# Attention rows without the first softmax's denominator, and the second softmax's factor made on GpSimd, in a two-layer hybrid encoder on one core

## The reference, cut to what matters

```python
s = jnp.einsum('bqhcd,bkhcd->bhcqk', qblk, kh) * scale
p = jax.nn.softmax(s, axis=-1)
p_diff = p[:, :, 0] - lam * p[:, :, 1]
o = jnp.einsum('bhqk,bkhv->bqhv', p_diff, vh)
...
o = rmsnorm(o, subln_g) * (1.0 - lam_init) * jax.nn.silu(g)
# rmsnorm(x, g) = x * rsqrt(mean(x * x) + 1e-6) * g
```

## Time and profile before

| what | value |
|---|---|
| median of 3 runs | 1490.94 us (1490.22 to 1490.95) |
| profiled execution: its time | 1490.54 us |
| profiled execution: span of its instructions | 1488.7 us |
| TensorE matmul busy | 1471.9 us, 11216 instructions |
| VectorE busy | 1047.2 us, 1787 instructions |
| ScalarE busy | 836.1 us, 1768 instructions |
| GpSimd busy | 90.5 us, 109 instructions |
| chain that ended last | TensorE 96%, VectorE 1%, ScalarE 1%, issue 1% |
| granted TensorE clock | 1.0 of full speed, over the whole span |

### The profile page before, as it was taken

The page is one execution under the profiler, slowest core; times in us unless marked ns, Lnnn a source line. Parts: engine busy times, 40 slices in busy tenths (PEclk is TensorE's granted clock), DMA queues, the critical chain, the costliest instruction groups (busy, mean ns, idle before and its releaser), DMA issues.

```text
span 1488.7 us, 28116 instructions
## 1 busy us (share of the span) xinstructions
PE 1471.9 (99%) x11216; PEld 1402.6 (94%) x11216; DVE 1047.2 (70%) x1787; ACT 836.1 (56%) x1768; POOL 90.5 (6%) x109
## 2 busy tenths in 40 slices
PE   7999999999999999999999999999999999999998
PEld 7999999999999999999999999999999889999987
DVE  7777667776664777777576676767776657777754
ACT  6565555665433565566555555566654445665654
POOL 0000000000000000000100000000001000000010
PEclk9999999999999999999999999999999999999999
DMA  6112111111223222222232121121212232222222
GB/s 208 63 53 66 64 58 57 58 57 58 76 68 89 84 72 72 72 66 67 69 101 86 57 72 57 62 68 57 71 58 72 72 104 82 72 72 82 76 84 73
DMA packets 34562, 109.94 MB, mean 74 GB/s; under 512 B 4864, under 2 KB 4992, under 8 KB 34432
## 3 DMA queue, kind: packets, MB, share of 16 engines
q1 hardware_dynamic: 34432, 108.15, 23.3%
HBM read 97.38 MB, written 2.10 MB: 67 GB/s over the span
## 4 chain that ended last, share of the span: by engine, by line
PE 96%; DVE 1%; ACT 1%; issue 1%; DMA 0%; SPq 0%; DVEq 0%; ACTq 0%
PE proj L1556 65%; PE pair L1674 8%; PE meta L1784 4%; PE pair L1769 2%; PE pair L1771 2%; PE main L1798 2%; PE meta L1786 1%; PE main L1739 1%; PE pair L1720 1%; PE main L1740 1%; PE main L1652 1%; PE main L1681 1%; PE main L1743 1%; PE pair L1727 1%; PE pair L1706 0%
## 5 line engine op out<-in xcount | busy, mean ns | idle before, releaser
L1556 PE MATMUL proj<-u_hi,w_hi 128*128 128x264 f32 (+1 forms) x2048 | 495.2, 313 | 9.0 <-DVE w_lo L1082 7.8
L1556 PE MATMUL proj<-u_hi,w_lo 128*128 128x264 f32 (+1 forms) x2048 | 465.6, 299 | 0.0
L1556 PE MATMUL proj<-u_lo,w_hi 128*128 128x264 f32 (+1 forms) x2048 | 465.3, 298 | 0.0
L1556 PEld LDWEIGHTS proj<-u_hi,w_hi 128*128 128x128 f32 x2048 | 327.2, 190 | 21.5 <-DVE w_lo L1082 7.8
L1556 PEld LDWEIGHTS proj<-u_hi,w_lo 128*128 128x128 f32 x2048 | 326.3, 189 | 11.2
L1556 PEld LDWEIGHTS proj<-u_lo,w_hi 128*128 128x128 f32 x2048 | 326.6, 189 | 7.7
L1082 DVE TENSOR_TENSOR w_lo<-w_raw,w_hi 128x1024 fp32r<-128x1024 f32 x178 | 218.9, 1230 | 51.3 <-ACT w_hi L682 51.3
L904 ACT ACTIVATE decay<-pair,neg_max 128x528 f32<-128x528 f32 (+1 forms) x144 | 100.3, 696 | 218.3 <-DVE neg_max L1423 218.1
L682 ACT ACTIVATE w_hi<-w_raw 128x1024 fp32r<-128x1024 f32 x178 | 186.6, 1049 | 53.0 <-PE proj L1556 51.8
L1423 DVE TENSOR_REDUCE neg_max<-pair 128x1 f32<-128x528 f32 (+1 forms) x144 | 101.4, 704 | 110.5 <-PE pair L1771 110.4
L1674 PE MATMUL pair<-q_level,qk_dec 128*128 128x128 f32 x896 | 121.4, 278 | 0.0
(11 more groups left out here) (216 smaller groups left out, 2214.4 us busy)
## 6 DMA issues: line engine op xcount, KB each, us to landing
w_raw<-w_units SPq DMA_DIRECT2D x178, 512.0 KB, 3.5
q_stack<-gate_f SPq DMA_DIRECT2D x32, 132.0 KB, 2.3
k_stack<-k_stack SPq DMA_DIRECT2D x32, 132.0 KB, 2.3
h<-x_t SPq DMA_DIRECT2D x8, 264.0 KB, 5.6
cos_sin<-rope SPq DMA_DIRECT2D x2, 528.0 KB, 6.1
out_t<-ops SPq DMA_DIRECT2D x2, 512.0 KB, 3.5
out_t<-decay SPq DMA_DIRECT2D x2, 512.0 KB, 3.9
masks<-level_masks SPq DMA_DIRECT2D x1, 448.0 KB, 6.4
```

The source lines that it names most:

```text
L1556: ins = pe.matmul(out, w, x[:, tile, cols_n], start=(k == 0 and p == 0), stop=(k == last_k and p == 2))
```

## The change

The copy of the attention result no longer scales a row by 1 / s0; for the attention heads the epsilon that invert_rms adds is multiplied by s0 squared, row by row (`square_sums`, into `eps_sums`). The factor -lam s0 / s1 is made on GpSimd (`relate_sums`: s1 to the power of -1, then times lam and s0), and VectorE waits for it (`ratio_ready`) where it made it itself. `row_sum` holds a head's sums for all blocks, twice, so that square_sums finds them. GpSimd's queue in an attention head becomes: relate_sums of block 0, cut_mixed of the head before, relate_sums of the other blocks, square_sums, invert_rms. Two memsets come at the start. The sums are set to 1.0 at the start, which is what stays where a block has no row.

```diff
@@ -365,14 +365,16 @@
         minus_half = sb("minus_half", [P, N_CHUNKS + 1])
+        minus_one = sb("minus_one", [P, 1])
         mixed_t = sb("mixed_t", [P, T])
...
         neg_max = sb("neg_max", [P, 2, 2])
-        row_sum = sb("row_sum", [P, 2, 2])
-        row_inv = sb("row_inv", [P, 2, 2])
+        row_sum = sb("row_sum", [P, 2, 2, N_CHUNKS + 1])
+        sum_ratio = sb("sum_ratio", [P, 2])
+        eps_sums = sb("eps_sums", [P, N_CHUNKS + 1])
 
@@ -480,6 +487,10 @@
 
+        def attended(n):
+
+            return n // HEADS * AT_HEADS + n % HEADS - HG_HEADS
+
         def evac_count(t):
@@ -632,22 +643,57 @@
             pool.memset(minus_half[:, :], -0.5).then_inc(ones_set, 1)
+            pool.memset(minus_one[:, :], -1.0).then_inc(ones_set, 1)
             pool.memset(v_meta[:, :], 0.0).then_inc(pads_set, 1)
...
             pool.memset(k_low[:, :, :].bitcast(f32), 0.0).then_inc(pads_set, 1)
+            pool.memset(row_sum[:, :, :, :], 1.0).then_inc(pads_set, 1)
 
...
                     pool.wait_ge(o_scaled, n)
-                pool.tensor_scalar(o_inv[:, :], o_sums[:, :], P * NORM_EPS, None, ALU.add)\
-                    .then_inc(pool_step, 1)
+                if n % HEADS < HG_HEADS:
+                    pool.tensor_scalar(o_inv[:, :], o_sums[:, :], P * NORM_EPS, None, ALU.add)\
+                        .then_inc(pool_step, 1)
+                else:
+                    pool.wait_ge(eps_ready, attended(n) + 1)
+                    pool.tensor_tensor(o_inv[:, :], o_sums[:, :], eps_sums[:, :], ALU.add)\
+                        .then_inc(pool_step, 1)
                 pool.wait_ge(pool_step, n + 1)
                 pool.tensor_tensor(o_inv[:, :], o_inv[:, :], minus_half[:, :], ALU.pow)\
                     .then_inc(o_inv_ready, 1)
+
+            def relate_sums(n, j):
+
+                l, a = n // HEADS, attended(n)
+                at = before(a, 5, AT_HEADS) + j
+                r = slice(0, P if j < N_CHUNKS else N_META)
+                if n == HG_HEADS and j == 0:
+                    pool.wait_ge(lam_ready, 1)
+                pool.wait_ge(exp_done, 2 * at + 2)
+                if at >= 2:
+                    pool.wait_ge(p_ready, at - 1)
+                s0, s1 = (row_sum[r, a % 2, comp, j:j + 1] for comp in range(2))
+                ratio = sum_ratio[r, at % 2:at % 2 + 1]
+                pool.tensor_tensor(ratio, s1, minus_one[r, :], ALU.pow).then_inc(sum_inverted, 1)
+                pool.wait_ge(sum_inverted, at + 1)
+                pool.tensor_scalar(ratio, ratio, lam[r, l:l + 1], s0, ALU.mult, ALU.mult).then_inc(ratio_ready, 1)
+
+            def square_sums(n):
+
+                a = attended(n)
+                pool.wait_ge(exp_done, 2 * before(a + 1, 5, AT_HEADS))
+                if a > 0:
+                    pool.wait_ge(pool_step, n)
+                sums = row_sum[:, a % 2, 0, :]
+                pool.tensor_tensor(eps_sums[:, :], sums, sums, ALU.mult).then_inc(sums_squared, 1)
+                pool.wait_ge(sums_squared, a + 1)
+                pool.tensor_scalar(eps_sums[:, :], eps_sums[:, :], P * NORM_EPS, None, ALU.mult)\
+                    .then_inc(eps_ready, 1)
 
@@ -657,10 +703,18 @@
             for l in range(DEPTH):
-                for c in range(HEADS):
+                for c in range(HG_HEADS):
                     n = l * HEADS + c
                     if c > 0:
                         cut_mixed(n - 1)
+                    invert_rms(n)
+                for c in range(HG_HEADS, HEADS):
+                    n = l * HEADS + c
+                    relate_sums(n, 0)
+                    cut_mixed(n - 1)
+                    for j in range(1, query_chunks(l)):
+                        relate_sums(n, j)
+                    square_sums(n)
                     invert_rms(n)
@@ -903,7 +957,7 @@
                                    ACT.Exp, bias=neg_max[0:rows, i % 2, comp:comp + 1],
-                                   accum_out=row_sum[0:rows, i % 2, comp:comp + 1]).then_inc(exp_done, 1)
+                                   accum_out=row_sum[0:rows, a % 2, comp, i:i + 1]).then_inc(exp_done, 1)
                 if s == 1:
@@ -913,8 +967,7 @@
                     act.wait_ge(pv_done, chunks_before + j + 1)
-                    inv = row_inv[0:rows, j % 2, 0:1]
-                    act.activation(o_rows[0:rows, j, :], meta[0:rows, 0:P], ACT.Copy, scale=inv)\
+                    act.activation(o_rows[0:rows, j, :], meta[0:rows, 0:P], ACT.Copy)\
                         .then_inc(pv_read if j < chunks - 1 else o_taken, 1)
@@ -947,8 +1000,8 @@
 
-            act.wait_ge(ones_set, 4)
-            act.wait_ge(pads_set, 5)
+            act.wait_ge(ones_set, 5)
+            act.wait_ge(pads_set, 6)
             load_root_table()
@@ -1072,9 +1125,10 @@
                                            math.sqrt(P) * (1.0 - init) * 0.5, None, ALU.mult))
-                step(dve.tensor_scalar(g_hg[:, :], g_hg[:, :], math.sqrt(P), None, ALU.mult))
+                dve.tensor_scalar(g_hg[:, :], g_hg[:, :], math.sqrt(P), None, ALU.mult).then_inc(lam_ready, 1)
                 w = step(dve.tensor_scalar(g_final[:, :], g_final[:, :], math.sqrt(D_MODEL), None, ALU.mult))
                 after(w)
+                dve.wait_ge(lam_ready, 1)
 
@@ -1438,18 +1492,12 @@
                     r = slice(0, P if j < 4 else N_META)
-                    dve.wait_ge(exp_done, 2 * chunks_before + 2 * j + 2)
-                    w = step(dve.reciprocal(row_inv[r, j % 2, :], row_sum[r, j % 2, :]))
-                    after(w)
-                    w = step(dve.scalar_tensor_tensor(row_inv[r, j % 2, 1:2], row_inv[r, j % 2, 1:2],
-                                                      lam[r, l:l + 1], row_sum[r, j % 2, 0:1],
-                                                      ALU.mult, ALU.mult))
                     if j >= 2:
                         dve.wait_ge(p_turned, chunks_before + j - 1)
-                    after(w)
+                    dve.wait_ge(ratio_ready, chunks_before + j + 1)
 
                     e0, e1 = decay[r, 2 * (j % 2), :], decay[r, 2 * (j % 2) + 1, :]
-                    dve.scalar_tensor_tensor(qk_dec[r, j % 2, 0, :], e1, row_inv[r, j % 2, 1:2], e0,
+                    dve.scalar_tensor_tensor(qk_dec[r, j % 2, 0, :], e1, sum_ratio[r, (chunks_before + j) % 2:(chunks_before + j) % 2 + 1], e0,
                                              ALU.mult, ALU.add).then_inc(p_ready, 1)
...
```

More of the change, by code:

```diff
@@ L414, in encoder_trunk @@
         o_inv_ready = sem("o_inv_ready")
+        lam_ready = sem("lam_ready")
+        ratio_ready = sem("ratio_ready")
+        sum_inverted = sem("sum_inverted")
+        sums_squared = sem("sums_squared")
+        eps_ready = sem("eps_ready")
         o_scaled = sem("o_scaled")
@@ L1584, in sum_squares @@
                 if n == 0:
-                    pe.wait_ge(ones_set, 4)
+                    pe.wait_ge(ones_set, 5)
                 pe.wait_ge(h_sq_added, (n + 1) * (KT - 2))
```

## The result

The changed kernel takes 1502.45 us (median of 6 runs, 1502.08 to 1503.24) against 1490.93 us before: a ratio of 1.0078, 95% interval 1.0065 to 1.0091. It is slower by 11.5 us where 5 us were forecast, and it lies inside the stated range (1491 to 1512). The profiled execution took 1502.42 us, its span is 1500.4 us.

A forecast was written before the change was run, and what follows sets the result against it. The prediction took TensorE, busy 99% of the span, as the bound. Its terms, 4.2 + 0.6 + 1.1 - 0.9 = +5.0 us on the profiled 1490.54 us, gave 1495.5, or 1496 for the median; range 1491 to 1512.

The forecast's parts named there:

- blocks 0, 2 and 4 are hidden: Factors of these blocks in attention heads: GpSimd's longer chain was to be covered by slack, at no cost.
- a flat power: Rival: GpSimd's power costs 1.20 us whatever its size; +19.6 us, so 1510.5; chance 0.24.
- block 1, heads 9 to 14: Both layers: block 1's power waits behind mix_lo on GpSimd, so TensorE stops 0.35 us, 12 times: 4.2 us.
- last block, layer 1: Heads 9 to 14: the power waits for VectorE's weight cut, qk_dec starts 0.18 us later, six times: 1.1 us.
- heads 15: Head 15 of layer 1: TensorE already waits behind this chain, so nearly the whole 0.73 us shift counts; 0.6 taken.
- heads 8: Head 8 of both layers: VectorE's gates start ahead of mix_lo and TensorE's stops go; gain 2 x 0.45 = 0.9 us.
- 0.24 + 0.19 = 0.43: Guessed time in us of GpSimd's one-element power: an add's time plus 0.19 us for one element.
- the 0.24 us of the five-element form: Guessed time of GpSimd's second new instruction per block, the one-element multiply, taken from the five-element add.
- between: Outcome between the 1496 forecast and the 1510.5 of a power costing 1.20 us at any size; chance 0.12.
- what I take as hidden: VectorE's row maximum after block 1's qk_dec: 0.7 us late, but TensorE needs its scores a full step later; no cost.
- the one in which nothing waits at the port: Rival: one-element GpSimd instructions don't wait for VectorE at the port; +1.1 us, 1492; chance 0.12 shared with a cheaper power.
- The rival in which a power holds VectorE for its whole length: And is flat too: block 2's rotary multiply waits about 1 us more, 7 us on top, 1518; chance 0.04.

The follow-up runs named there:

- e4_slack: The changed kernel with idle powers added on GpSimd, of one element ahead of blocks 0 and 2 in heads 9 to 15, larger in head 8: 1502.89 us.
- e1_order: The changed kernel with cut_mixed behind block 1's ratio on GpSimd in heads 9 to 15: 1492.51 us, ratio 1.0013 to the kernel before.
- e3_port: The changed kernel with VectorE's weight cut of step 7 behind the rotary turn of step 8, heads 9 to 14 of layer 1: 1499.94 us.
- e2_vector: The changed kernel with the factor made by VectorE as before, the first denominator still moved into the epsilon: 1489.78 us, ratio 0.9995 to the kernel before.

## Why the prediction was right or wrong, point by point

**Direction and mechanism: right.** Every step that was named is in the trace: block 1 waits behind mix_lo 12 times, the last block of layer 1 waits for the weight cut at the port, the stops of head 8 go, blocks 0, 2 and 4 are hidden. The size was not: it is less than half of what was measured, and the time is inside the range because the range reached to a flat power of 1.20 us, which isn't what happened.

**Size: 5.0 us forecast, 11.5 measured.** The terms, with what each measured:

| term | forecast | measured |
|---|---|---|
| block 1, heads 9 to 14 | 12 x 0.35 = 4.2 | 12 x 0.73 = 8.8 |
| last block, layer 1 | 6 x 0.18 = 1.1 | 6 x 0.48 = 2.9 |
| heads 15 | 0.6 (layer 1 alone) | 1.0 (0.5 in each layer) |
| heads 8 | -0.9 | -1.3 |
| sum | 5.0 | 11.4 |

For block 1 the 8.8 is the 0.72 us that a head of layer 0 lost, and what a head of layer 1 lost over its last block, 1.23 - 0.48 = 0.75. In layer 0 it is a net figure: matmul by matmul against the kernel before, TensorE falls back 0.54 us before the transposes and 0.23 us before the scores of step 7, and gets 0.08 us back at the head's last product. Head 15 of layer 0 was put at nothing without a reason, and lost 0.5 us like that of layer 1. Two steps were at fault. The first is the price of the two instructions, "0.24 + 0.19 = 0.43" and "the 0.24 us of the five-element form". The excess over an add was spread over the elements alone; e4_slack shows that 0.38 us of a power are fixed, more than the whole add, and a multiply by two factors from tiles takes 0.34 us. That is 0.21 us more in each chain, and it was bounded, not foreseen: the point lay at the cheap end of a range of 0.24 to 1.20 us, and 1502 lies where the prediction put "between". The second is the step "what I take as hidden": that the row maximum, 0.7 us late, had a full step's room. The row maximum of the next step had; the one after it, behind four rotary instructions that VectorE works off without a break, didn't, and left TensorE idle for 0.17 us (0.10 in layer 1) before the scores of step 7. e1_order removes both with one edit.

**The last block.** The forecast had the power end 0.26 us after the weight cut and qk_dec start 0.61 us after it (1271.04 against 1270.43); before it was 0.43. Measured are 0.40 us for the power, 0.11 to the multiply, 0.34 for it and 0.11 to VectorE: qk_dec starts 0.96 us after the cut's end (1276.97 against 1276.01). The stop grew by 0.48 us, not 0.18. The part that was read from mix_lo was small but off: its 1.52 us were compared with the 1.32 us of one with 528 elements, while those with its own 512 take 1.28 us undisturbed, so that it had run beside VectorE's instruction for 0.14 us and not 0.17, just as the new power does.

**The rival of a flat power** (1510) fell, as did the one in which nothing waits at the port (e3_port). The rival in which a power holds VectorE for its whole length has nothing for it. In head 8, layer 0, a power is issued during a shuffle on VectorE, which has one input, and isn't held up (0.56 us); 0.43 us into it VectorE starts a rotary multiply of two SBUF inputs, which takes 0.71 us as ever. Rows 12 are the same for a power of five elements.

```profile
419.56 0.71 DVE L1287 TENSOR_TENSOR stage<-stage,cos_sin 128x528 f32<-128x528 f32 x1
...
419.13 0.56 POOL L682 TENSOR_TENSOR sum_ratio<-row_sum,minus_one 128x1 f32<-128x1 f32 x1 [5.26 <-ACT decay L958]
```

The Trainium skill, SBUF — State Buffer, section "Who interferes with whom", is thus borne out for the two directions in which GpSimd waits for VectorE and VectorE for mix_lo (1.52 us for 0.77), but not for a power.

**ScalarE's copy, put at nothing:** dropping its scale did save 0.09 us a block. In layer 0 ScalarE runs from that copy to the last turned block without a break, and TensorE gets 0.08 us a head for it, 0.5 us in heads 9 to 14. That is about half of e2_vector's small lead (1.0 us by the marks, 0.8 by the medians); most of what heads 9 to 14 of layer 1 add, 0.35 us, is the shorter way from multiply to qk_dec on VectorE.

## What to carry to other kernels

Where one engine is busy for 99% of the span, work taken off another pays only where the first one waits for it: of the 27 us taken off VectorE, the two stops at head 8, about 1 us, came back. Moving a small step of a chain to an idle engine pays or costs by what stands ahead of it in that engine's queue. Look up that queue in the trace, and put the step that someone waits for ahead of the one that has time; here this alone was 10 us. When a step comes late, follow the late engine's queue past the next step, until it idles. And a weight load's idle time shows where TensorE stops, but what the stop costs is the distance between matmuls with it and without it.

## What the runs showed of the hardware

- A power on GpSimd took 0.38 us and 0.16 us more for each element of a partition (0.54 us for one, 1.20 us for five).
- A power of one element on GpSimd, issued while VectorE ran an instruction with two SBUF inputs, ended 0.40 to 0.41 us after that one's end (39 times; 1.09 us instead of 0.54 in the last blocks of layer 1). Beside a VectorE instruction with one input, or with one of two in PSUM, it wasn't held up (0.55 to 0.56 us). It didn't hold up a VectorE instruction that started in the midst of it, where mix_lo with its 528 elements did (qk_dec 1.52 us instead of 0.77). Why the two differ is open.
- ScalarE's copy of 128 x 128 from PSUM took 0.25 to 0.28 us with a constant scale and 0.34 to 0.37 us with the scale from a tile.
